# Stick-breaking attention turn: values two steps behind their scores instead of three

## The reference, cut to what matters

```python
def sb_block(qb, qpos, k, v):
    kpos = jnp.arange(k.shape[2])
    z = jnp.einsum('bhtd,bhsd->bhts', qb, k) * SB_SCALE
    mask = (kpos[None, :] < qpos[:, None])[None, None]
    log_keep = jnp.where(mask, jax.nn.log_sigmoid(-z), 0.0)
    after = lax.cumsum(log_keep, axis=3, reverse=True) - log_keep
    w = jnp.where(mask, jnp.exp(jax.nn.log_sigmoid(z) + after), 0.0)
    return jnp.einsum('bhts,bhsd->bhtd', w, v)
```

## Time and profile before

| | us |
|---|---|
| median of 3 runs | 2735.16 (2728.69 to 2737.92) |
| profiled execution, its own time | 2731.04 |
| its span, first to last instruction | 2729.3 |
| TensorE busy | 2623.7 (96%) |
| VectorE busy | 1523.8 (56%) |
| ScalarE busy | 835.6 (31%) |
| GpSimd busy | 346.5 (13%) |
| mean granted TensorE clock | 0.979 of full |

### The profile page before, as it was taken

The page is one execution under the profiler, slowest core; times in us unless marked ns, Lnnn a source line. Parts: engine busy times, 40 slices in busy tenths (PEclk is TensorE's granted clock), DMA queues, the critical chain, the costliest instruction groups (busy, mean ns, idle before and its releaser), DMA issues. The chain is left out here.

```text
span 2729.3 us, 47931 instructions
## 1 busy us (share of the span) xinstructions
PE 2623.7 (96%) x17088; PEld 2498.5 (92%) x17088; DVE 1523.8 (56%) x2584; ACT 835.6 (31%) x1563; POOL 346.5 (13%) x327
## 2 busy tenths in 40 slices
PE   6999999999979999999979999999999999999997
PEld 6888888888869989899979999999999999999897
DVE  4665766676664756666663443454444445444754
ACT  4443443343432434334341122211111111111513
POOL 0222322222221111111100002100000000000300
PEclk8999999999988989999979999999999999999999
DMA  5444544465522242335345433411111111111112
GB/s 137 90 108 75 117 85 100 86 85 104 111 55 40 33 99 29 97 33 78 53 169 187 169 99 125 160 40 46 38 46 38 45 40 40 44 38 46 35 38 81
DMA packets 331857, 214.35 MB, mean 79 GB/s; under 512 B 117828, under 2 KB 312216, under 8 KB 331672
## 3 DMA queue, kind: packets, MB, share of 16 engines
q1 hardware_dynamic: 331672, 211.98, 32.7%
HBM read 164.51 MB, written 47.41 MB: 78 GB/s over the span
## 5 line engine op out<-in xcount | busy, mean ns | idle before, releaser
L165 PE MATMUL bank<-operand_hi,w_hi 128*128 128x384 f32 x1584 | 533.1, 337 | 1.5 <-DVE w_lo L148 1.5
L165 PE MATMUL bank<-operand_hi,w_lo 128*128 128x384 f32 x1584 | 530.2, 335 | 0.0
L165 PE MATMUL bank<-operand_lo,w_hi 128*128 128x384 f32 x1584 | 530.2, 335 | 0.0
L139 ACT ACTIVATE w_hi<-w_raw 128x1024 fp32r<-128x1024 f32 (+1 forms) x167 | 172.6, 1034 | 780.8 <-PE bank L165 486.6
L165 PEld LDWEIGHTS bank<-operand_hi,w_hi 128*128 128x128 f32 x1584 | 297.6, 188 | 2.1 <-issue 1.8
L165 PEld LDWEIGHTS bank<-operand_lo,w_hi 128*128 128x128 f32 x1584 | 297.7, 188 | 0.3
L165 PEld LDWEIGHTS bank<-operand_hi,w_lo 128*128 128x128 f32 x1584 | 297.5, 188 | 0.0
L685 PE MATMUL acc<-operand_hi,w_hi 128*128 128x384 f32 x792 | 281.2, 355 | 5.5 <-PEq L215 5.5
L1057 POOL TENSOR_TENSOR wgt<-wgt,left 128x128 f32<-128x128 f32 (+2 forms) x224 | 210.7, 946 | 573.9 <-DVE left L1014 413.6
L148 DVE TENSOR_TENSOR w_lo<-w_raw,w_hi 128x1024 fp32r<-128x1024 f32 (+1 forms) x167 | 201.6, 1207 | 138.8 <-ACT w_hi L139 137.7
L165 PE MATMUL sacc<-operand_hi,w_hi 128*128 128x384 f32 x768 | 268.7, 350 | 6.3 <-DVE w_lo L148 6.3
(11 more groups left out here) (355 smaller groups left out, 4477.5 us busy)
## 6 DMA issues: line engine op xcount, KB each, us to landing
w_raw<-in_w_in SPq DMA_DIRECT2D x65, 512.0 KB, 8.0
k_cache<-in_cache_k SPq DMA_DIRECT2D x256, 64.0 KB, 2.7
v_cache<-in_cache_v SPq DMA_DIRECT2D x64, 256.0 KB, 4.6
w_raw<-in_w_gate SPq DMA_DIRECT2D x22, 512.0 KB, 3.8
w_raw<-in_w_up SPq DMA_DIRECT2D x22, 512.0 KB, 3.8
w_raw<-in_w_down SPq DMA_DIRECT2D x22, 512.0 KB, 3.8
s_gate_a<-gate SPq DMA_DIRECT2D x24, 192.0 KB, 3.0
s_o<-o_t SPq DMA_DIRECT2D x8, 576.0 KB, 9.3
```

What stands on the lines that cost most here:

```text
L139: act.activation(hi, S.raw[u0 % 2][:, 0:cols], ACT.Copy).then_inc(S.hi_done, 1)
L165: last = pe.matmul(acc[:, 0:RBN], w[:, k, :], a[:, k, rows], start=(n == 0), stop=(n == 3 * kts - 1 and more is None))
```

## The change

One constant. The values of a double unit are done two steps behind its scores instead of three.

```diff
 UNITS = [u for d in range(ND) for u in units_of(d)]
 NU = len(UNITS)
-LAG = 3
+LAG = 2
 STEPS = ND + LAG
 SLOTS = 2 * STEPS
 S_AT = [d for d in range(ND) if DU[d][0] == "s"]
```

## The result

The changed kernel took 2770.32 us (median of 4 runs, 2765.98 to 2774.55), the kernel before 2734.6 us beside it. The ratio is 1.0139, 95% interval 1.0113 to 1.0165: slower by 1.4%. 2771 was predicted, in a range of 2754 to 2789.

The account below looks back on a forecast made before the run. TensorE, busy 96% of the span, was taken to bound the kernel. Values' waits 27, last turn 5 and store 8, less 1.5 for the missing step, gave 38.5 us more: 2771 us predicted, range 2754 to 2789.

Parts of the forecast that it names:

- The values' wait: In seven attention turns, TensorE's values wait for VectorE's copies of their transposed weights: 3.9 us a turn, 27 us.
- the missing step: One step fewer per attention turn saves its cost beyond its work: 0.2 us a turn, 1.5 us in all.
- Step 9: Values wait behind VectorE's v2 row copies; 0.2 us taken as v2 is turned earlier, 0.75 for the high end.
- The last turn: Half the products, VectorE already late: waits for the copies of 5 us, 3 to 7.
- The store: ScalarE's read into o_t, moved to step 2, waits for the o_t store and holds TensorE: 8 us, 0 to 16.
- rival A: Store landings late in most turns; the six other turns pay some 4 us instead of 0.5: 2791 us, chance 0.06.
- The sum: 27 + 5 + 8 - 1.5 = 38.5 us over the kernel before, predicted at 2771 us.
- B: Half hidden: VectorE finishes its copies earlier, so only steps 14 and 15 wait: 2750 us, chance 0.08.
- C: TensorE's clock falls at each turn's end, 2.4 us per swing, 19 us: 2790 us, chance 0.03.
- D: Not slower: a step costs more beyond its work, 0.76 us each, and copy waits are absent: 2725 to 2733, 0.10.
- The signs: Expected profile: turns some 98 us, two waits at turn's end, one hole in step 3, TensorE busy time unchanged, clock 1.00.

Follow-up runs that it names:

- the even spread alone: Kernel before (values three steps behind) with the product pieces spread over the first 32 of 34 slots, three in each: 2735.3 us, ratio 1.0009.
- the early store: Changed kernel with SP issuing the store of o_t ahead of the turn's last weight load: 2754.0 us, ratio 1.0080.
- cover for the last two steps: Changed kernel with the values behind the first slot of products in steps 14 and 15: 2754.9 us, ratio 1.0080.
- 17 steps: Changed kernel, values two steps behind, but the turn keeps 17 steps and 34 product slots as before: 2775.1 us, ratio 1.0157.
- the longer copy: Changed kernel with an unused reduction ahead of VectorE's copy of each second unit's transposed weights: 2816.0 us, ratio 1.0304.
- cover in all steps: Changed kernel with the values behind the first slot of products in every step: 2751.7 us, ratio 1.0078.

## Why the prediction was right, point by point

**The values' wait** was 3.9 us a turn in the prediction. The distances from the transposes' start to the values, after less before, in the second turn:

| step | predicted | measured |
|---|---|---|
| 2 | 0.27 | 0.29 |
| 4, 7, 10 | 0.2, 0.25, 0.25 | 0.22, 0.25, 0.12 |
| 5 | 0.28 | 0.25 |
| 6 | 0.1 | 0.05 |
| 9 | 0.2 | 0.56 |
| 14 | 1.26 | 1.28 |
| 15 | 1.07 | 1.02 |

Their sum is 4.0. A turn grew by 96.73 - 92.89 = 3.84. The difference to 4.0 is about the 0.2 us that I gave to the missing step, but the even spread alone showed 0.17, and no run separates the two.

**Step 9 was the miss** within it. I took v2's earlier turn for relief. It was turned earlier, but VectorE wasn't free. The low part of a weight tile (1.23 us at 224.51) had moved one step forward, ahead of this step's scans, and v2's two copies began only at 229.18, right behind them, and the second took 0.97 us where it had taken 0.43. I had noted that the splits move and let 0.5 us of it be slack, which it was for the scans and not for the copies behind.

**The last turn** was put at 5 us: from its first transposes to the stage end it took 79.0 us against 74.0. Of the 5.0 us 0.6 is a held read.

**The store** was put at 8 us with 0 to 16. The mechanism is as described. In the turn that begins at 664 the store is issued at 668.6, lands 13.9 us later, and the next values wait for ScalarE's read:

```profile
682.61 0.28 ACT L923 ACTIVATE o_t<-o 128x128 f32<-128x128 f32 x1 [6.81 <-DMA s_o<-o_t]
```

```profile
679.54 0.11 PEld L740 LDWEIGHTS z<-mask_prompt,ident_bf 128*128 128x128 bf16 x2 [0.37 <-issue]
683.00 0.45 PEld L778 LDWEIGHTS o<-w_t,v_rows 128*64 128x64 f32 x8 [3.35 <-issue]
```

Behind this hole the clock falls to the 1.2 GHz level. The busy times by stretch, columns as in the earlier trace rows:

```profile
680.00:684.00 4.00, 0.97 (x10) 0.83 (x11) 0.32 (x1) 1.39 (x4) 0.00 (x0) 0.97 1.04 357
684.00:687.00 3.00, 3.00 (x12) 3.00 (x11) 3.00 (x4) 1.78 (x5) 1.09 (x1) 0.50 0.72 177
687.00:690.00 3.00, 3.00 (x22) 2.77 (x21) 1.63 (x3) 0.63 (x3) 1.09 (x1) 0.97 0.54 123
```

12 matmuls in 3 us at 0.50, 22 in the next 3 us at 0.97: some 1.5 us lost on top of the hole, which is 3.20 us in the matmul row (3.35 in the weight loads). The first nine product matmuls behind it take 2.96 us, the next nine 1.67. The two together explain why this turn was 4.75 us longer than with the early store.

The term measured 6.2 us: 4.75 and 0.89 in the lengths of two turns and 0.57 in the last one. The holds themselves are 3.20, 0.76 and 0.57, or 4.5 us; the rest is mostly the clock, which the prediction had at 1.00. So the 4.9 us given to the first of these turns agree with 4.75 partly by luck, and the two others, given 1.7 each, were over-sized.

The landings were misread. The first line of the earlier trace rows also covers eight loads of `s_o` by later stages; the eight stores alone, before and after, are:

```profile
DMA to landing us min/median/max: 7.1/9.3/14.5
...
DMA to landing us min/median/max: 7.1/9.6/13.9
```

Nothing of the term's 8 us hangs on the median, only the weight against rival A.

**The sum** in the profiled executions: the seven turns grew by 31.2 us (25.6 without the 5.6 of the holds, against 27 - 1.5 predicted), the last by 5.0, and the start was 0.5 shorter: 35.7 of the 38.5 foreseen. The spans differ by 40.0. The other 4.3 us lie in the later stages, whose code is unchanged; in the other profiled executions these took 1914 to 1926 us, in no order of the kernels, so I don't count it to the change. That prediction and median agree to 1 us is partly luck: the terms were 3 us too large, and the base they were added to was 1.6 us under the median of before as it stood with the fourth run.

**The rivals.** A (late landings everywhere) didn't come: the median is 9.6 us against 9.3, and three stores of eight held TensorE, though ScalarE waited for six. B is refuted by the distances, nine of which grew. C is refuted for the turn's end, where I had put it: the clock in the turn is 1.00 with two gaps of 1.2 us in it. The Trainium skill (TensorE: Matmul & The Clock Gate, section "A second HAM failure mode: psum-queue depth-cycling") warns that frequent short idle moments between groups of matmuls make the clock swing; gaps of this size did not. The fall came once, behind the held read, where I had not looked for it. D: what a step costs beyond its work is 0.2 us or less, not 0.76 or more.

**The signs.** A turn with the loop's way back grew from 94.4 to 97.9 us (98 predicted), the two waits at the turn's end and the hole in step 3 are there. Two signs were off: TensorE's busy time was to stay the same and grew by 13.4 us, and the clock fell once.

## What to carry to other kernels

On the engine that sets the time, a shorter software pipeline saves only the joins of the step that falls away (here at most 0.2 us a turn). Before shortening, lay the end of the helper's work beside the moment of its use in the place that the use will have, and look at the last steps, where the work that would cover it has run out. Follow also the reads that move forward with it to the buffer that they fill: its last store may not have landed. And look at what SP has queued ahead of a stage's last store, as all engines wait for it; here one reordered DMA was worth 12 us in the kernel before, where the missing step could give 1.5.

## What the runs showed that was not expected

- The end of a stage waited for the last store: 12.9 us on TensorE, 3.8 with the store issued one DMA earlier, and 12 us of the whole time (ratio 0.9952). Some 9.6 of it is seen at the stage end; the rest is within the interval.
- A hole of 3.20 us in TensorE's matmul row was followed by some 3 us at the 1.2 GHz level. So were the held read's holes of 3.98 us with cover for the last two steps and of 4.24 us with 17 steps, and the 2.99 us at the way back with the spread alone. The gaps of 1.2 us were not, nor, in the kernel with the longer copy, those of up to 1.85 us in the weight loads. Yet a hole of 2.98 us at the held read of that kernel left the clock at 1.00, and one of 2.18 us with cover in all steps was followed by 0.54 over 3 us. So here the length of a hole alone doesn't tell whether the clock falls behind it.
- The loop's way back costs TensorE 1.0 to 1.6 us in the kernels whose turn ends in 9 or more matmuls of products, and 5.6 us in the one whose turn ends in values, 2.6 of them by the clock. Why the gap is longer there was not tried.
- Another run of products costs 0.16 us by the division above, where the mean lengths of the earlier trace rows gave 0.1 us.
- The stages behind the pairs vary by 12 us between executions (granted clock 0.972 to 0.979 over the span) with the same code, a third of the effect measured here. A difference of a few microseconds is only readable from the turns themselves.
